# One input array for the constants, and an activation on 16 columns in place of 2048

## The reference, cut to what matters

```
c_act = jax.nn.silu(c)                       # (1, 2048)
mod = c_act @ w_ada[l] + b_ada[l]            # w_ada is 2048 x 12288
sh_a, sc_a, gt_a, sh_f, sc_f, gt_f = [m[:, None, :] for m in jnp.split(mod, 6, axis=-1)]
h = _rmsnorm(x, norm_mix[l]) * (1.0 + sc_a) + sh_a
p = h @ w_in[l]
```

## Time and profile before

| what | value |
|---|---|
| time before, median of 3 | 2245.32 us (2245.22 to 2245.76) |
| the profiled execution | 2242.18 us |
| its span in the trace | 2240.9 us |
| TensorE busy, share of the span | 98% |
| VectorE busy | 67% |
| ScalarE busy | 44% |
| mean granted TensorE clock | 0.993 |

### The profile page before, as it was taken

One profiled execution on the slowest core, in us unless ns is written; L12 is line 12 of the kernel. 1 busy time (PEld: TensorE's weight loads), 2 busy tenths in 40 slices (PEclk: granted clock), 3 DMA queues, 4 the chain that ended last, 5 costly groups with the idle time before them and its releaser, 6 DMA issues.

```text
span 2240.9 us, 27231 instructions
## 1 busy us (share of the span) xinstructions
PE 2188.2 (98%) x10552; PEld 1837.0 (82%) x10552; DVE 1502.1 (67%) x1882; ACT 994.4 (44%) x1259; POOL 25.9 (1%) x28
## 2 busy tenths in 40 slices
PE   7899999999999999999999999999999999999998
PEld 5788988788888888888888888888888888888886
DVE  7988798778988676765545555576556655655555
ACT  4356444333444554443444434465444444444444
POOL 0001000000000000000000000000000000000000
PEclk9999999999999999999999999999999999999999
DMA  9984667886899678876655556565666566566663
GB/s 373 420 292 142 206 199 265 271 265 235 293 336 322 232 242 289 295 238 198 191 189 188 190 195 190 186 207 187 194 192 192 185 193 196 186 189 193 193 191 123
DMA packets 249523, 507.87 MB, mean 227 GB/s; under 512 B 26633, under 2 KB 43057, under 8 KB 243889
## 3 DMA queue, kind: packets, MB, share of 16 engines
q1 hardware_dynamic: 249394, 506.13, 67.9%
HBM read 503.56 MB, written 2.51 MB: 226 GB/s over the span
## 4 chain that ended last, share of the span: by engine, by line
PE 83%; DVE 8%; DMA 5%; ACT 2%; issue 1%; SPq 0%; POOL 0%; DVEq 0%; ACTq 0%
PE bank L1229 26%; PE bank L1231 26%; PE bank L1230 26%; DVE WL L2013 2%; PE bank L1420 1%; DVE RAW L2000 1%; PE bank L1161 1%; DMA RAW<-in_w_ada_dram 1%; DVE A L2193 1%; ACT WH L1499 1%; DMA A<-in_w_cq_dram 1%; DMA RAW<-in_w_cd_dram 1%; DMA A<-in_w_cd_dram 1%; DMA RAW<-in_w_cq_dram 1%; PE bank L1236 1%
## 5 line engine op out<-in xcount | busy, mean ns | idle before, releaser
L2013 DVE TENSOR_TENSOR WL<-RAW,WH 128x1024 fp32r<-128x1024 f32 x706 | 859.9, 1223 | 583.1 <-ACT WH L1499 578.1
L1499 ACT CAST WH<-RAW 128x1024 fp32r<-128x1024 f32 x706 | 738.7, 1050 | 876.2 <-PE bank L1231 718.2
L1229 PE MATMUL bank<-WH,HTh 128*128 128x512 f32 x1922 | 758.0, 394 | 3.0 <-DVE WL L2013 3.0
L1231 PE MATMUL bank<-WH,HTl 128*128 128x512 f32 x1922 | 749.7, 390 | 0.0
L1230 PE MATMUL bank<-WL,HTh 128*128 128x512 f32 x1922 | 749.2, 390 | 0.0
L1229 PEld LDWEIGHTS bank<-WH,HTh 128*128 128x128 f32 x1922 | 361.4, 188 | 77.6 <-DVE WL L2013 3.8
L1231 PEld LDWEIGHTS bank<-WH,HTl 128*128 128x128 f32 x1922 | 361.2, 188 | 76.1
L1230 PEld LDWEIGHTS bank<-WL,HTh 128*128 128x128 f32 x1922 | 361.6, 188 | 72.6
L1229 PE MATMUL bank<-WH,R2h 128*128 128x512 f32 x408 | 160.9, 394 | 4.6 <-DVE WL L2013 2.7
L1231 PE MATMUL bank<-WH,R2l 128*128 128x512 f32 x408 | 159.6, 391 | 0.0
L1230 PE MATMUL bank<-WL,R2h 128*128 128x512 f32 x408 | 159.5, 391 | 0.0
(11 more groups left out here) (286 smaller groups left out, 1819.7 us busy)
## 6 DMA issues: line engine op xcount, KB each, us to landing
RAW<-in_a_w_in_dram SPq DMA_DIRECT2D x192, 512.0 KB, 3.7
RAW<-in_w_gate_up_dram SPq DMA_DIRECT2D x176, 512.0 KB, 4.5
RAW<-in_w_ada_dram SPq DMA_DIRECT2D x128, 512.0 KB, 5.6
RAW<-in_w_in_dram SPq DMA_DIRECT2D x112, 512.0 KB, 5.2
RAW<-in_w_down_dram SPq DMA_DIRECT2D x88, 512.0 KB, 4.6
RAW<-in_a_w_out_dram SPq DMA_DIRECT2D x64, 512.0 KB, 4.4
A<-in_w_ada_dram SPq DMA_DIRECT2D x17, 1024.0 KB, 14.1
RAW<-in_w_o_dram SPq DMA_DIRECT2D x32, 512.0 KB, 6.6
```

What stands on the lines that cost most here:

```text
L1229: e.matmul(o, ah[:, s], hi[:, k, :], start=first, stop=False)
L1231: i = e.matmul(o, al[:, s], hi[:, k, :], start=False, stop=last)
L1499: e.copy(hi, rv).then_inc(S["hi"], 1)
L2013: e.tensor_tensor(lo, rv, hi.bitcast(F32), ALU.subtract).then_inc(S["lo"], 1)
```

## The change

One array `cst` now carries everything small. Its first part, 576 columns, holds the identity, the ones, the frequencies, COL, the positions and `c` as 16 columns; its second part, 920 columns instead of 776, holds the rest of the constants and the three vectors, repeated to all partitions by the host. The transfers of `c`, `positions`, COL, `A_log`, `dt_bias` and `gdn_norm` are gone. The activation is taken on the 16 columns of `c`. VectorE multiplies the identity with each of these columns, which gives 16 diagonal blocks (CD, 128x2048), and TensorE multiplies ones (128x128) with CD, so that each bank holds silu(c) (twice over) on all partitions. ScalarE copies two of the banks to CB and VectorE the other two.

```diff
@@ front
         self.put("load_x")
         self.issue_loads(5)
-        self.put("load_vec")
         self.issue_loads()
         m = self.ms()
-        for n in range(4):
-            if n == 3:
-                self.put("x_sq", 1)
-                self.put("x_rs", m)
-            self.put("c", n)
-            if n == 0:
-                self.put("x_sq", 0)
+        self.put("x_sq", 0)
+        self.put("c", 0)
+        self.put("c", 1)
+        self.put("x_sq", 1)
+        self.put("c", 2)
+        self.put("c", 3)
+        self.put("x_rs", m)
@@ TensorE
         if kind == "begin":
-            W.wait_ge("c_in", 16)
             W.wait_ge("cst_in", 16)
             for n in range(4):
-                e.matmul(bank[n], ones[0:1, :], L.crow[:, 512 * n:512 * n + 512], start=True, stop=True).then_inc(S["c_t"], 1)
+                W.wait_ge("c_d", n + 2)
+                e.matmul(bank[n], ones, L.CD[:, 512 * n:512 * n + 512], start=True, stop=True).then_inc(S["c_t"], 1)
@@ ScalarE
-        if kind == "c":
+        if kind == "begin":
+            W.wait_ge("cst_in", 16)
+            e.activation(L.cth, L.ccol, ACT.Tanh, scale=0.5).then_inc(S["c_th"], 1)
+
+        elif kind == "c" and args[0] < 2:
             n, = args
             W.wait_ge("c_t", n + 1)
-            e.activation(L.TH[:, 512 * n:512 * n + 512], bank[n], ACT.Tanh, scale=0.5).then_inc(S["c_th"], 1)
+            e.copy(L.CB[:, 512 * n:512 * n + 512], bank[n]).then_inc(S["cact"], 1)
@@ VectorE
         if kind == "begin":
-            W.wait_ge("cols_in", 32)
+            W.wait_ge("cst_in", 16)
+            W.wait_ge("c_th", 1)
+            e.scalar_tensor_tensor(out=L.csil, in0=L.cth, scalar=1.0, in1=L.ccol, op0=ALU.add, op1=ALU.mult
+                                   ).then_inc(S["c_d"], 1)
+            W.wait_ge("c_d", 1)
+            for n in range(4):
+                e.tensor_tensor(L.CD[:, 512 * n:512 * n + 512].rearrange("p (k j) -> p k j", j=P), bm4(L.ident),
+                                bc4(L.csil[:, 4 * n:4 * n + 4]), ALU.mult).then_inc(S["c_d"], 1)
@@ VectorE, step load_cst2 (the same edit stands in sm_b, and in ScalarE's sm_c)
         elif kind == "load_cst2":
-            W.wait_ge("vec_in", 48)
+            W.wait_ge("cst_in", 32)
             e.tensor_scalar(L.gn, L.gn, 0.5, None, ALU.mult).then_inc(S["cols"], 1)
@@ SyncE
         if kind == "begin":
-            e.dma_start(L.crow, a["c"]).then_inc(S["c_in"], 16)
             e.dma_start(L.CST[:, 0:C_TRI], a["cst"][:, 0:C_TRI]).then_inc(S["cst_in"], 16)
-            with L.nc.allow_non_contiguous_dma(reason="256 positions"):
-                e.dma_start(L.posi, a["positions"].rearrange("a (b p) -> p (a b)", p=P)).then_inc(S["cols_in"], 16)
-            e.dma_start(L.COL[:, 0:256], a["cols"]).then_inc(S["cols_in"], 16)
-        elif kind == "load_vec":
-            e.dma_start(L.al, spread_row(a["A_log"], 8)).then_inc(S["vec_in"], 16)
-            e.dma_start(L.dtb, spread_row(a["dt_bias"], 8)).then_inc(S["vec_in"], 16)
-            e.dma_start(L.gn, spread_row(a["gdn_norm"], P)).then_inc(S["vec_in"], 16)
```

More of the change, by code:

```diff
@@ L20 @@
 KB = 256
-C_ID, C_ONE, C_INV, C_NH, C_TRI, C_PAIR, C_OFF, C_CM, C_BM, C_ID16, C_END = 0, 128, 256, 288, 296, 424, 552, 680, 808, 816, 1072
+C_ID, C_ONE, C_INV, C_NH, C_COL, C_POS, C_C, C_TRI, C_PAIR = 0, 128, 256, 288, 296, 552, 554, 576, 704
+C_OFF, C_CM, C_BM, C_ID16, C_AL, C_DT, C_GN, C_END = 832, 960, 1088, 1096, 1352, 1360, 1368, 1496
 CS = 3 * P + 80
@@ L170, in __init__ @@
         self.CST = self.place("CST", C_END)
-        self.COL = self.place("COL", 256)
         self.MOD = self.place("MOD", 96)
@@ L182, in __init__ @@
         self.A = self.place("A", 100 * KB)
-        self.posi = nc.alloc_sbuf_tensor_at("posi", [P, 2], I32, offset=self.at)[:, :]
-        self.at += 32
-        self.gn = self.place("GN", P)
         self.ROPE = self.place("ROPE", 320)
@@ L194, in __init__ @@
         self.pair, self.off, self.bm = C[:, C_PAIR:C_PAIR + P], C[:, C_OFF:C_OFF + P], C[:, C_BM:C_BM + 8]
-        c = self.COL
+        self.posi, self.ccol = C[:, C_POS:C_POS + 2].bitcast(I32), C[:, C_C:C_C + 16]
+        self.gn = C[:, C_GN:C_GN + P]
+        c = self.COL = C[:, C_COL:C_COL + 256]
         self.colNM, self.colNF, self.colAN = c[:, 192:208], c[:, 208:224], c[:, 224:240]
@@ L203, in __init__ @@
         self.neg_half = C[:, C_NH:C_NH + 8]
-        self.al, self.dtb, self.eA = s(8), s(8), s(8)
+        self.al, self.dtb, self.eA = C[:, C_AL:C_AL + 8], C[:, C_DT:C_DT + 8], s(8)
+        self.cth, self.csil = s(16), s(16)
         self.cAm, self.cAf, self.posf, self.rs1, self.ss1 = s(16), s(16), s(2), s(2), s(2)
@@ L233, in __init__ @@
         self.X = two(0, 2 * D)
-        self.crow, self.TH, self.SQ1 = ar(16, 2048)[0:1, :], ar(56, 2048), two(64, 4096)
+        self.CD, self.SQ1 = ar(16, 2048), two(64, 4096)
         self.XS1, self.CS = two(16, 4096), [ar(36, 1024), ar(96, 1024)]
@@ L1167, in pe_program @@
         if kind == "begin":
-            W.wait_ge("c_in", 16)
             W.wait_ge("cst_in", 16)
             for n in range(4):
-                e.matmul(bank[n], ones[0:1, :], L.crow[:, 512 * n:512 * n + 512], start=True, stop=True).then_inc(S["c_t"], 1)
-                held[n // 2] = [("cact", 1 + n)]
+                W.wait_ge("c_d", n + 2)
+                e.matmul(bank[n], ones, L.CD[:, 512 * n:512 * n + 512], start=True, stop=True).then_inc(S["c_t"], 1)
+                held[n // 2] = [("cact", 4)]
         elif kind == "xt":
@@ L1917, in rope_tables @@
     def rope_tables():
-        W.wait_ge("cst_in", 16)
         e.tensor_copy(L.posf, L.posi).then_inc(S["angle"], 1)
@@ L1979, in dve_program @@
                 next(tables)
-        elif kind == "c":
+        elif kind == "c" and args[0] > 1:
             n, = args
[L1983 to L1986, removed]
+            W.wait_ge("c_t", n + 1)
+            e.tensor_copy(L.CB[:, 512 * n:512 * n + 512], bank[n]).then_inc(S["cact"], 1)
             for _ in range(6 if n == 2 else 0):
@@ L2750, in program @@
     pool_program(nc.gpsimd, L, S, sch)
-_LAYER = ("w_in", "w_uq", "w_ukv", "w_o_mla", "A_log", "dt_bias", "gdn_norm", "w_o_gdn", "w_o", "w_gate_up", "w_down",
+_LAYER = ("w_in", "w_uq", "w_ukv", "w_o_mla", "w_o_gdn", "w_o", "w_gate_up", "w_down",
           "a_w_in_2", "a_v_gain_2", "a_w_s_2", "a_w_out_2")
-_WHOLE = ("c", "positions", "final_norm", "final_norm_2")
+_WHOLE = ("final_norm", "final_norm_2")
 def columns(inputs):
@@ L2762, in columns, with constants @@
     return np.concatenate(parts).T
+def constants(inputs):
+    k = shape_constants()
+    k[:, C_COL:C_COL + 256] = columns(inputs)
+    k[:, C_POS:C_POS + 2] = np.asarray(inputs["positions"]).astype(np.int32).reshape(2, P).T.copy().view(np.float32)
+    k[:, C_C:C_C + 16] = np.asarray(inputs["c"]).reshape(16, P).T
+    for at, name in ((C_AL, "A_log"), (C_DT, "dt_bias"), (C_GN, "gdn_norm")):
+        v = np.asarray(inputs[name]).reshape(1, -1)
+        k[:, at:at + v.shape[1]] = v
+    return k
 def modulation(w):
@@ L2783 @@
     nc = _bacc.Bacc("TRN2", target_bir_lowering=False, num_devices=1, dynamic_dma_scratch_size=1024)
-    host = {"x": np.asarray(inputs["x"])[0], "cst": shape_constants()}
-    host["cols"] = columns(inputs)
+    host = {"x": np.asarray(inputs["x"])[0], "cst": constants(inputs)}
     host["w_ada"] = modulation(np.asarray(inputs["w_ada"])[0])
```

## The result

| | before | after |
|---|---|---|
| median | 2245.32 us (2245.12 to 2245.76, 5 runs) | 2255.16 us (2250.25 to 2256.38, 5 runs) |
| ratio, 95% interval | | 1.0041 [1.0028, 1.0054] |
| profiled execution, span | 2242.18, 2240.9 | 2255.16, 2253.9 |
| granted TensorE clock | 0.993 | 0.988 |

The changed kernel is slower by 9.8 us, beyond the upper end of the forecast range. The traces of the two profiled executions show the forecast itself at 146 us, and then a loss in a part of the program that no step of the change touches.

A forecast was written before the change was run, and what follows sets the result against it. The prediction took the first 130 us to be bound by transfers, DMA engines full. -4.35 (front) + 6.6 (wait at the halving) = +2.25 on 2242.18 gives 2244.4, plus 3.1 to the median: 2247.6 us, range 2243.2 to 2251.4.

The forecast's parts named there:

- the forecast itself: Front gain of 4.35 us and a 6.6 us wait at the gain's halving, sum +2.25 us; given 60%.
- The front, -4.35: Transfers up to about 130 us: removing the three vectors' loads (2.76) and an earlier start (1.6) saves 4.35 us.
- Both thin stretches: Slow transfers at 1.5 to 5 us (140 GB/s) and 21.5 to 25.5 us (149 GB/s), laid to small loads.
- Rival B: The front gains only what VectorE gains, the dip not being the vectors' doing: 2250.5 to 2251.2 us; chance 14%.
- VectorE's first product, -0.75: At the start, the first product comes some 0.75 us earlier, at 13.0; counted as nothing beside the transfers' 4.35.
- The wait at the halving, +6.6: End of the front: VectorE's halving of the gain waits for the constants' second part, delaying the convolution 6.6 us.
- Rival A: The wait at the halving costs nothing, so the front's gain stands alone: 2241.0 us; chance 10%.
- The sum at 146 us: Front and wait together at the convolution near the end of the front: -4.35 + 6.6 = +2.25 us.
- the signs: Trace marks named beforehand, among them VectorE idle 6 to 11 us before the halving and TensorE pausing over 6 us.
- Rival C, the clock: TensorE's clock falls after its new pause of 6.4 us, mean +1.7 us, so 2249.3 us; chance 16%.
- The step that failed: Arena A, holding matmul tiles, moves by 672 bytes in each partition; priced at nothing.

The follow-up runs named there:

- e3: The changed kernel with 88 unused words ahead of arena A and the three vectors in the constants' first part; 2237.79 us, ratio 0.9971 to the kernel before.
- e4: The kernel before with the three vectors as one host array loaded by one transfer; 2240.74 us, ratio 0.9987.
- e2: The changed kernel with 88 unused words ahead of arena A, putting A 1,024 bytes from its old place; 2243.47 us, ratio 0.9999 to the kernel before.
- e1: The kernel before with 168 unused words ahead of arena A, so A starts 672 bytes later; 2252.2 us against 2243.55, ratio 1.0036.

## Why the prediction was wrong

- **The front, -4.35.** Right in kind: the last product is 3.8 earlier, 0.55 less than forecast, and the convolution in e3 4.6 earlier. Both thin stretches filled up, one by the vectors (e4). Rival B is out. The 6.0 us that the prediction estimated from the Trainium skill's "DMA: Bandwidth & Descriptors", "Anatomy of one DMA", is not borne out: the three vectors cost 1.65 us in e4's trace and 2.8 in the medians. That section is on transfers that GpSimd issues; these are SyncE's.
- **VectorE's first product, -0.75, worth nothing.** Right in kind: -0.59, while the last product gained 3.8, taken out of VectorE's idle time (9.8 us in 100 became 5.8).
- **The wait at the halving, +6.6.** Right in mechanism and near in size: e3's convolution is 6.89 earlier than that of the kernel after, of which 0.62 stand at the last product already (129.24 and 129.86); the wait itself is 6.3. Against the kernel before it is 6.1 (from the last product to the convolution 16.89 for 10.83). Its issue was priced at 139.70 less 4.35 or 135.35, it came at 135.87, and the load took 8.45 for 8.8. Rival A is out; e3 measures what A would have been had the wait cost nothing, 5.8 us faster than before.
- **The sum at 146 us.** Its +2.26 for the forecast 2.25 is luck in the last digit: the front gave 0.55 less and the wait took 0.55 less. TensorE paused for 5.5 us where the signs named over 6. And the forecast's own range, 2246.3 to 2249.5, is not what the bounds of its terms give; they add up to +1.2 and +5.6, or 2246.5 to 2250.9.
- **What of it goes through.** VectorE at 175.97 became 178.25, +2.28: nothing was caught up by 178 us.
- **Rival C, the clock.** It is there, beside the forecast rather than in its place. The window after the pause:

```profile
140.00:150.00 10.00, 4.50 (x23) 4.30 (x22) 5.66 (x10) 4.29 (x9) 0.00 (x0) 0.66 0.61 215
```

  Up to 178 us it costs VectorE nothing. Behind that the distance of VectorE's low parts of the weights grows from 2.3 us at 176 to 3.8 at 190, 5.5 at 251 and 6.6 at 325, and is 5.2 at 499. The granted clock falls to 1.2 GHz at 181, 201 and 310 us in the profiled execution after, and at 180, 306, 408 and 432 us in the one before, and the fall at 181 lasts longer than that at 180 (mean clock from 181 to 190: 0.63). That these falls are the 3 us is argued from their places, not measured. They differ from one execution to the next: 24 runs of the kernel before on one chip lie between 2240.34 and 2246.80.

  All five executions of the kernel after have a lower mean clock, 0.987 to 0.990, and e2 has 0.989 to 0.992. Part of it lies in the pause, and part in the front, from 5 to 25.5 us (0.76 and 0.50 in the windows), where the transfers set the pace. e2 has both, the one in the front shorter, and is no slower than the kernel before, so the lower mean is not the 9.8 us. Whether the change makes the clock fall more often behind 178 us stays open: after and e2 both have a fall near 201 us that the traces of before, e1 and e3 lack, but e4 has one near 198.
- **The step that failed** reads: "The arena A moves by 672 bytes in each partition. No row prices an address; I take nothing." It measured +8.1 (e1), and taking it out again gave 2243.47 (e2), where the rest of the forecast, +2.25, would be 2245.8, just beyond that interval's upper end of 0.08%. The sum by the steps that held and by e1 is 2.25 + 8.1 = 10.3; measured 9.8, with an interval from 6.3 to 12.1. The sentence was true of the rows shown, but then the bounds of this term had to be wide or the address had to be given a rival of its own: the change moved a tile of 1,032 recorded matmuls of the down projections and of some 190 others. e2 also leaves open how much of the +2.25 reached the end: by its median 0, with an interval from -2.2 to +1.8.

## What to carry to other kernels

When a constant array grows, look at what lies behind it: on this kernel the arrays of activations and of weights that the matmuls read cost nothing when one of them moves by 256, 512 or 1,024 bytes against the other, and 5 to 7 ns for each matmul of 512 columns when it moves by 32, 64, 96, 128 or 672. The old places are multiples of 256 bytes apart; that every such multiple is safe is inferred from these. A window in which TensorE is 100% busy in both kernels, at the same clock, with fewer matmuls in one of them, is the sign of it; no wait shows it. And a load that is merged into a later one is to be placed by its earliest reader: the three vectors cost 1.7 us (trace) to 2.8 us (medians) of transfers as they were, 6.3 us as part of a late array, and nothing in the first part of the constants.

## What was not expected of the hardware

- The distance of the arrays that the matmuls read, within 256 bytes: 389 ns for a 128x512 matmul's record (WL with aTh) at 0, 395 to 398 at all others that were tried, and 2.72 against 2.80 us for 12 of them in a row. Why it is so, no run here shows, nor whether it lies between the tiles of one matmul or of two that follow each other; distances that are no multiple of 32 bytes were not tried.
- Three row-repeating transfers of 72 KB in all hold the queue at 149 GB/s for 4 us and take 16.7 to 18.0 us to land; one plain transfer of the same bytes leaves 429 GB/s there.
- A GpSimd instruction of 0.70 us takes 2.83 us when it meets a product on VectorE, without any effect on the end here.
